# Thirty-two bytes less ahead of the shared SBUF regions of a two-layer decoder kernel

## The reference

```python
for i in range(2):
    x = x + 0.5 * swiglu_ffn(rmsnorm(x, n_ffn1[i]), ffn1_w_gu[i], ffn1_w_down[i])   # d_ff = 2816
    h = rmsnorm(x, n_mix[i])
    x = x + (gla_mixer(h, ...) if i == 0 else pool_mixer(h, ...))
    x = x + mem_cross_attn(rmsnorm(x, n_xattn[i]), rmsnorm(mem, n_mem[i]), x_w_q[i], x_w_kv[i], x_w_o[i])
    x = x + 0.5 * swiglu_ffn(rmsnorm(x, n_ffn2[i]), ffn2_w_gu[i], ffn2_w_down[i])
return rmsnorm(x, n_final)

def swiglu_ffn(h, w_gu, w_down):
    g, u = jnp.split(h @ w_gu, 2, axis=-1)
    return (jax.nn.silu(g) * u) @ w_down
```

## The kernel before

| tensor | start | modulo 64 | modulo 1024 |
|---|---|---|---|
| x, h_hi, h_lo, raw, w_hi, w_lo | 16512 + n x 16384, n = 0 to 5 | 0 | 128 |
| rms_tok | 116864 | 0 | 128 |
| t, sq | 118944, 123040 | 32 | 160 |
| ident (identity matrix) | 127136 | 32 | 160 |
| cols | 129216 | 0 | 192 |
| phase | 129664 | 0 | 640 |
| start of the regions (mid_hi, o_hi, x_tok, y_tok) | 130176 | 0 | 128 |

## Time and profile before

### The profile page before, as it was taken

How to read it: one execution, slowest core, us unless ns; L and a number is a source line. 1 busy time by engine, 2 the same in 40 slices (tenths; PEclk the granted TensorE clock), 3 DMA queues, 4 the chain that set the end, 5 groups by cost and what they waited for, 6 DMA issues and landing times.

```text
span 2025.2 us, 24246 instructions
## 1 busy us (share of the span) xinstructions
PE 2013.7 (99%) x9756; PEld 1695.9 (84%) x9756; DVE 920.2 (45%) x998; ACT 714.9 (35%) x870; POOL 99.9 (5%) x105
## 2 busy tenths in 40 slices
PE   9999999999999999999999999999999999999998
PEld 7888888898898988888888888888898888888887
DVE  4343333487665544343333433442276544343333
ACT  5232222366654533232222422232156443222222
POOL 1000001000011020000000000010002010000000
PEclk9999999999999999999999999999999999999999
DMA  5323322221332333323323223222343123323231
GB/s 170 104 83 103 98 99 90 87 84 63 105 113 96 110 101 102 104 83 103 99 94 99 95 92 104 91 90 94 98 144 108 62 83 104 103 83 104 94 99 57
DMA packets 193275, 197.12 MB, mean 97 GB/s; under 512 B 3602, under 2 KB 191632, under 8 KB 193216
## 3 DMA queue, kind: packets, MB, share of 16 engines
q1 hardware_dynamic: 191360, 192.69, 29.4%
q0 software_dynamic: 960, 2.29, 0.4%
q10 hardware_dynamic: 896, 1.32, 0.2%
HBM read 194.18 MB, written 2.10 MB: 97 GB/s over the span
## 4 chain that ended last, share of the span: by engine, by line
PE 96%; ACT 1%; DVE 1%; DMA 0%; issue 0%; ACTq 0%
PE ps L316 32%; PE ps L318 32%; PE ps L317 31%; ACT w_hi L1037 0%; DMA raw<-in_ffn_w_gu 0%; DVE w_lo L1513 0%; PE ps L800 0%; PE ps L763 0%; PE ps L559 0%; ACT y_tok L1503 0%; PE ps L578 0%; PE ps L749 0%; PE ps L556 0%; DVE qk_lo L1513 0%; ACT p_tok L1286 0%
## 5 line engine op out<-in xcount | busy, mean ns | idle before, releaser
L316 PE MATMUL ps<-h_hi,w_hi 128*128 128x512 f32 (+1 forms) x1728 | 670.1, 388 | 1.4 <-DVE q L1779 0.4
L317 PE MATMUL ps<-h_lo,w_hi 128*128 128x512 f32 (+1 forms) x1728 | 666.1, 385 | 0.0
L318 PE MATMUL ps<-h_hi,w_lo 128*128 128x512 f32 (+1 forms) x1728 | 666.1, 385 | 0.0
L1513 DVE TENSOR_TENSOR w_lo<-raw,w_hi 128x2048 fp32r<-128x2048 f32 (+4 forms) x194 | 416.9, 2149 | 468.2 <-ACT w_hi L1037 468.1
L1037 ACT ACTIVATE w_hi<-raw 128x2048 fp32r<-128x2048 f32 (+4 forms) x194 | 347.3, 1791 | 259.0 <-PE ps L318 254.7
L316 PEld LDWEIGHTS ps<-h_hi,w_hi 128*128 128x128 f32 x1728 | 324.9, 188 | 67.8 <-issue 2.6
L317 PEld LDWEIGHTS ps<-h_lo,w_hi 128*128 128x128 f32 x1728 | 324.9, 188 | 65.5 <-issue 1.2
L318 PEld LDWEIGHTS ps<-h_hi,w_lo 128*128 128x128 f32 x1728 | 324.8, 188 | 65.3
L316 PE MATMUL ps<-mid_hi,w_hi 128*128 128x512 f32 x704 | 274.0, 389 | 0.0
L318 PE MATMUL ps<-mid_hi,w_lo 128*128 128x512 f32 x704 | 273.9, 389 | 0.0
L317 PE MATMUL ps<-mid_lo,w_hi 128*128 128x512 f32 x704 | 273.9, 389 | 0.0
(11 more groups left out here) (329 smaller groups left out, 1761.2 us busy)
## 6 DMA issues: line engine op xcount, KB each, us to landing
raw<-in_ffn_w_gu SPq DMA_DIRECT2D x87, 1024.0 KB, 5.0
raw<-in_ffn_w_down SPq DMA_DIRECT2D x32, 1024.0 KB, 5.2
raw<-in_x_w_kv SPq DMA_DIRECT2D x16, 1024.0 KB, 5.5
raw<-in_ffn_w_down SPq DMA_DIRECT2D x16, 768.0 KB, 4.4
raw<-in_gla_w_in SPq DMA_DIRECT2D x12, 1024.0 KB, 5.1
raw<-in_x_w_q SPq DMA_DIRECT2D x8, 1024.0 KB, 5.2
raw<-in_x_w_o SPq DMA_DIRECT2D x8, 1024.0 KB, 5.2
raw<-in_gla_w_out SPq DMA_DIRECT2D x8, 512.0 KB, 3.4
```

The source lines that it names most:

```text
L316: nc.tensor.matmul(out_ap, left[0], right[0], start=first, stop=False)
L317: nc.tensor.matmul(out_ap, left[0], right[1], start=False, stop=False)
L318: return nc.tensor.matmul(out_ap, left[1], right[0], start=False, stop=last)
L1513: return nc.vector.tensor_tensor(out_ap, value, hi.bitcast(F32), ALU.subtract)
```

## The change

One number changes: the filler `phase` has 120 columns of float32 in place of 128.

```diff
@@ -187,7 +187,7 @@
             return col(name, layer * C + c)
 
 
-        sb("phase", [P, 128])
+        sb("phase", [P, 120])
 
         def region(name, offset, shape, dt=F32):
             with ExitStack() as e:
```

## The result

The changed kernel takes 2043.38 us (median of 4 runs, 2042.64 to 2044.03), against 2026.85 us for the kernel before on the same chip. The ratio is 1.0081, with a 95% interval of 1.0063 to 1.0099. It is slower by 16.5 us. The forecast was 2027.0 us with a range up to 2042, so the time lies outside the range, and the likeliest case, no effect, did not come.

A forecast was written before the change was run, and what follows sets the result against it. The prediction took a row of TensorE matmuls of fixed spacing as the bound. Its terms, 0 + 0 + 0 for TensorE, VectorE and ScalarE, head and tail, left 2027.0 us, with a range of 2020 to 2042.

The forecast's parts named there:

- the likeliest case: Whole kernel: no effect, edges included, with its own range of 2024 to 2030 us; chance 0.68.
- What bounds the kernel: Whole kernel: a row of TensorE matmuls of fixed spacing, TensorE busy 2013.7 of 2025.2 us and 96% of the path.
- The TensorE term: About 3,350 matmuls whose moving operands shift by 32 bytes: cost taken as 0.
- The bounds of 45 us: Shifted matmuls: a second fixed 13.3 ns on 3,350 gives +45 us; loss of the fixed part gives -45 us.
- The identity rows: Transposes moving the identity matrix, 32 bytes past a multiple of 64: 109 and 111 ns spacing, read as no penalty.
- I see no place on which it depends: Groups on mid, xo and o: weight slices 512 bytes apart show means of 389 to 393 ns, no second value.
- The surplus is per instruction: All matmuls: each carries a fixed 13.3 ns beyond its columns, at 512 columns (226.7 ns) and 256 (120.0 ns).
- the second rival: Large matmul groups: fixed part is two streams in step; shifting saves 2 ns each, -7 us, 2020 us; chance 0.12.
- The first rival: Shifted matmuls, mainly down projections: start off a 64-byte boundary costs 3.3 ns each, +11 us, 2038 us; chance 0.20.
- VectorE, ScalarE, head and tail: Other engines and the kernel's two ends: instruction durations and DMA of x_tok and y_tok unchanged, each taken as 0.
- the bound given for the edges: Head and tail: shifted DMA packets a tenth faster or slower would change the time by 0.7 us either way.
- The signs to look for: For the first rival: spacing up on mid, xo, o equally; h unchanged; span surplus equal to that number times 3,350.

The follow-up runs named there:

- the kernel with 64 bytes more: Filler phase with 144 columns in place of the 128 of the kernel before, so all regions start 64 bytes higher: 2032.41 us, ratio 1.0026.
- the trace with h slower at its own old address: 32 bytes of filler ahead of w_hi in the kernel before, moving weights and regions while h stays: 2056.69 us, ratio 1.0144.

## Why the prediction was wrong, point by point

*What bounds the kernel:* right. A row of matmuls on one engine with nothing to hide behind: what the distances between the starts gained, 17.0 us, the span gained too. But not all 3,350 shifted matmuls gained the same.

*The TensorE term, "I take 0":* this is the step that failed. It measured +6.6 ns on the 2,688 matmuls that move mid, xo and o, some 17.6 us, and took back about 1 us on 256-column groups. The bounds of 45 us held it; the choice within them did not. Two readings led to it. The identity rows are fp32 matmuls of 128 columns; they were taken as a measure of fp32r matmuls with 512. The traces show that they are none. The row over p_tok lies at D = 32 before and at 64 after the change, and at -32 in the kernel with 64 bytes more; its pace is 109.0 ns in all three. The row of 111 ns is a second thing again: its weights are one value of rms_tok, repeated for all 128 columns. The row over p_tok after the change:

```profile
678.90 1.03 PE L800 MATMUL ps<-ident,p_tok 128*128 128x128 f32 x8
```

And "I see no place on which it depends" came from groups that all had D = 0, with slices a whole number of 256-byte periods apart: equal paces at equal distances say nothing about other distances. The list of starts modulo 256 would have shown that the trace held no test of what the change did.

*"The surplus is per instruction":* wrong as a fixed 13.3 ns. It was read from two points, 226.7 and 120.0 ns. The lowest paces found were 226.7, 173.3 and 113.3 ns for 512, 384 and 256 columns, which is 13.3, 13.3 and 6.7 ns over one column a cycle, and the 120.0 had a place surplus in it. With it fell the size of the second rival's gain: at 512 columns there was nothing to win below 226.7.

*The first rival,* slower through a moving operand off a 64-byte boundary, had the right sign and place, mid above all. Its mechanism is refuted by the kernel with everything moved (ratio 0.9996) and the one with 64 bytes more (1.0026), and its price of 3.3 ns was half of the 6.7 measured. *The second rival* named the right quantity, moving operand and weights in or out of step, with the wrong sign for 512 columns; for 256 it was right, -1.7 ns on m. Its price of 2 ns came from those two identity rows, whose weights are read in different ways. I argued against it with slices 512 bytes apart, which are two whole periods. The sign of the first rival and the quantity of the second belonged together.

The Trainium skill (SBUF — State Buffer, Specifications) gives lines of 16 bytes, and a cost for crossing into a new one. I let it lower the first rival's chance; the runs show a period of 256 bytes in the distance of two operands, of which that rule gives no sign, and a cost at whole multiples of 32 bytes. The Trainium skill (SBUF — State Buffer, SBUF: two separate sides) says that TensorE's SBUF port never waits on anyone; as far as ScalarE and VectorE go, the program with both busy agrees, with at most 0.1 ns between the settled paces of any line.

*VectorE, ScalarE, head and tail:* right. 688, 633 and 623 ns against 688, 632 and 623; the last store is issued 3.8 us before the end of the span, 3.7 before. The first 25 us lost 0.8 us of busy time, about the bound given for the edges. The kernel with everything moved (21.84 us busy there) and the one without the filler (21.88) have the same head, with spans of 2025.2 and 2025.6 us, so it costs the end nothing.

*The signs to look for:* they worked in part. Spacing on mid up, that on h unchanged, and the surplus the same in mid, xo and o were signs given for the first rival, and they came. The third did not: 6.6 ns times 3,350 is 22 us, and the span grew by 17.0, since 256-column groups at the same shift did not slow. That alone spoke against a price on every moving operand off a 64-byte boundary; the trace with h slower at its own old address settled it.

## What to carry to other kernels

Where TensorE is the bound and matmuls follow each other without a gap, the byte distance between the starts of the moving operand and the weights, modulo 256, is a property of the kernel: write it down for every large group before padding, reordering or resizing any SBUF tensor. For fp32r, 512 columns and 128 weight columns take 0, with both starts on multiples of 32 bytes: of the four places that were entered in eight ways it alone came back to the fastest pace every time. Of the other fast ones, -16, -20 and 108 had a slower pace as well in another program, and -4, 28 and 60 lost 1.5 to 3 ns when the matmuls walked through tiles. And before taking "no row shows an effect" as evidence, see whether any two rows differ in the quantity that the change alters.

## What the runs showed of the hardware that was not expected

- Matmuls in fp32r with 512 columns and 128 weight columns, one after another with a new weight load each, the weights on a multiple of 32 bytes: 226.7 ns at D = 0, about 233.3 at 32 and -32, up to 240 at odd multiples of 4, with a period of 256 bytes. Never under 226.7. With 256 columns: 113.3 at the best places, 120.0 at D = 0.
- Transposes by fp32 matmuls of 128 columns: 109.0 ns at D = 32, 64 and -32 alike.
- A steady pace is not a function of the addresses alone: D = -16 held 226.7, 233.3 or 237 ns for 24 matmuls, by what ran ahead, and in the decoder 226.7 or 233.3 for about 1,000 matmuls.
- Below 32 bytes a common shift of both operands counts as well: 231.1 ns with both 16 bytes on, 237.8 with both 4 bytes on, 226.7 with both 32 on.
- No run beat the kernel before. The gains seen are on 256 columns only: 120.4 to 116.0 ns for m at D = 64, 0.8 us for its 190 intervals, too little to be told from no change; moving such pairs alone was not tried beyond the kernels above. What in the chip makes the period of 256 bytes, and the several lasting paces, is left open.
